# Gate of each layer: the residual's second half transposed on VectorE and moved by direct on-chip transfers, first projection unit between the gate's second and third unit

## The reference, cut to what matters

```python
h = h + mix                                            # the mixer's output
h = h + swiglu(rms_norm(h, norm_ffn[i]), ffn_w_in[i], ffn_w_out[i])
gate = jax.nn.sigmoid(rms_norm(h, ple_norm[i]) @ ple_w_gate[i])     # 1024 x 1024
h = h + gate * (p[i] @ ple_w_proj[i])                                # 256 x 1024
```

## Time and profile before

| what | value |
|---|---|
| median of three runs | 903.44 us (903.12 to 903.55) |
| the profiled execution's own time | 902.82 us |
| its span (first to last instruction) | 900.6 us |
| TensorE matmuls | busy 893.0 us (99%), 4358 instructions |
| VectorE | busy 654.4 us (73%), 995 instructions |
| ScalarE | busy 508.0 us (56%), 821 instructions |
| GpSimd | busy 62.3 us (7%) |
| SyncE's DMA queue | 182.99 MB, 60.2% of 16 engines |
| granted TensorE clock | 1.000 of full speed in the whole span |

### The profile page before, as it was taken

The page is one execution under the profiler, slowest core; times in us unless marked ns, Lnnn a source line. Parts: engine busy times, 40 slices in busy tenths (PEclk is TensorE's granted clock), DMA queues, the critical chain, the costliest instruction groups (busy, mean ns, idle before and its releaser), DMA issues.

```text
span 900.6 us, 12222 instructions
## 1 busy us (share of the span) xinstructions
PE 893.0 (99%) x4358; PEld 737.1 (82%) x4358; DVE 654.4 (73%) x995; ACT 508.0 (56%) x821; POOL 62.3 (7%) x75
## 2 busy tenths in 40 slices
PE   9999999999999999999999999999999999999998
PEld 8988888888888888778888888888888888887776
DVE  5985478777735699997787776646679897779663
ACT  6756555444444667688564444435664645587681
POOL 0001000000000003211100000000010000225100
PEclk9999999999999999999999999999999999999999
DMA  7674459777755666424487777746658775657611
GB/s 260 202 240 140 168 189 303 270 242 243 240 195 193 225 201 203 161 95 139 141 291 257 234 246 246 250 147 224 212 204 284 254 259 185 217 204 235 227 52 47
DMA packets 76844, 187.47 MB, mean 208 GB/s; under 512 B 6836, under 2 KB 31540, under 8 KB 76792
## 3 DMA queue, kind: packets, MB, share of 16 engines
q1 hardware_dynamic: 75336, 182.99, 60.2%
q0 software_dynamic: 1024, 3.15, 1.0%
q10 hardware_dynamic: 432, 0.66, 0.2%
HBM read 171.83 MB, written 14.94 MB: 207 GB/s over the span
## 4 chain that ended last, share of the span: by engine, by line
PE 94%; DMA 2%; DVE 2%; ACT 1%; issue 1%; ACTq 0%; DVEq 0%
PE bank L1792 84%; PE bank L1819 3%; DMA raw<-stream_dram 2%; PE bank L1834 1%; PE bank L2094 1%; PE bank L2120 1%; DVE wlo L1077 1%; PE bank L2204 1%; DMA h<-x_dram 0%; PE bank L2105 0%; PE bank L1941 0%; PE bank L1989 0%; PE bank L1993 0%; PE bank L2080 0%; PE bank L2214 0%
## 5 line engine op out<-in xcount | busy, mean ns | idle before, releaser
L669 ACT ACTIVATE whi<-raw 128x1024 fp32r<-128x1024 f32 x295 | 306.5, 1060 | 181.7 <-DMA raw<-stream_dram 104.6
L1077 DVE TENSOR_TENSOR wlo<-raw,whi 128x1024 fp32r<-128x1024 f32 x295 | 347.8, 1214 | 53.9 <-ACT whi L669 53.2
L1792 PE MATMUL bank<-whi,x_hi 128*128 128x512 f32 x560 | 152.5, 394 | 0.0
L1792 PE MATMUL bank<-wlo,x_hi 128*128 128x512 f32 x560 | 149.9, 389 | 0.0
L1792 PE MATMUL bank<-whi,x_lo 128*128 128x512 f32 x560 | 149.7, 389 | 0.0
L1792 PEld LDWEIGHTS bank<-wlo,x_hi 128*128 128x128 f32 x560 | 105.1, 188 | 22.1
L1792 PEld LDWEIGHTS bank<-whi,x_lo 128*128 128x128 f32 x560 | 105.1, 188 | 22.0
L1792 PEld LDWEIGHTS bank<-whi,x_hi 128*128 128x128 f32 x560 | 103.4, 188 | 21.8 <-issue 1.2
L1792 PE MATMUL bank<-whi,y_hi 128*128 128x512 f32 x400 | 109.5, 394 | 0.0
L1792 PE MATMUL bank<-wlo,y_hi 128*128 128x512 f32 x400 | 107.6, 389 | 0.0
L1792 PE MATMUL bank<-whi,y_lo 128*128 128x512 f32 x400 | 107.5, 389 | 0.0
(11 more groups left out here) (244 smaller groups left out, 886.0 us busy)
## 6 DMA issues: line engine op xcount, KB each, us to landing
raw<-stream_dram SPq DMA_DIRECT2D x295, 512.0 KB, 4.5
ffn_blocks<-ffn_blk SPq DMA_DIRECT2D x22, 256.0 KB, 2.0
ffn_land<-ffn_blocks SPq DMA_DIRECT2D x22, 256.0 KB, 4.0
second_blocks<-h_blk SPq DMA_DIRECT2D x8, 256.0 KB, 2.0
h_land<-second_blocks SPq DMA_DIRECT2D x8, 256.0 KB, 3.0
cv_blocks<-cv_blk SPq DMA_DIRECT2D x7, 256.0 KB, 5.2
cv_land<-cv_blocks SPq DMA_DIRECT2D x7, 256.0 KB, 3.5
h_blocks<-h_blk SPq DMA_DIRECT2D x3, 512.0 KB, 6.5
```

The lines of the kernel that those rows point to most:

```text
L669: A(whi[:, u % RING, :], raw[:, u % RAW, :], ACT.Copy).then_inc(sem("w_hi"), 1)
L1077: V.tensor_tensor(wlo[:, u % RING, :], raw[:, u % RAW, :], whi[:, u % RING, :].bitcast(F32), ALU.subtract).then_inc(sem("w_lo"), 1)
L1792: last = T.matmul(bank[pair + t][:, :], lhs[a][:, kt, t * P:(t + 1) * P], w[:, u % RING, kk * NW:(kk + 1) * NW], start=part != 1 and k == ...
```

## The change

The second half of the residual reaches the gate by blocks instead of through TensorE, and the blocks are moved inside the chip: `cross` issues four transfers for one piece, each from 32 partitions of `h_blk` (2 KB each) to 128 partitions of `h_land` (512 B each), 64 KB in all, with no DRAM tensor in between. The same transfers replace the way over DRAM in `second_blocks` (four uses before, six now) and in `gate_blocks` (two). The first half for the gate (`half_blocks`) still goes over DRAM. The units of `tple` and `tple+1` are made in the order of `GATE_ORDER`: gate 0, gate 1, projection, gate 2, gate 3.

```diff
+GATE_ORDER = ((0, 0), (0, 1), (1, 0), (0, 2), (0, 3))
...
+            for tile in (PLE0, PLE1):
+                for n, (t, k) in enumerate(GATE_ORDER):
+                    SOURCE[END[tile] + n] = END[tile + t] + k
...
+            def cross(dst, src, signal):
+                for i in range(P // B):
+                    sp.dma_start(dst[:, i, :], src[i * B:(i + 1) * B, :]).then_inc(sem(signal), 16)
...
                 for q in range(2):
                     sp.wait_ge(sem("g_blk"), 2 * r + q + 1)
-                    sp.dma_start(s_dram[s, q], sblk[:, q, :]).then_inc(sem(f"g_out{q}"), 16)
-                for q in range(2):
-                    sp.wait_ge(sem(f"g_out{q}"), 16 * (r + 1))
-                    sp.dma_start(sland[:, q, :, :], s_dram[s, q].rearrange("q n -> (q n)")
-                                 .rearrange("(i p w) -> p i w", i=P // B, p=P)).then_inc(sem(f"g_land{q}"), 16)
+                    cross(sland[:, q, :, :], sblk[:, q, :], f"g_land{q}")
...
                 for t in range(TT):
-                    sp.wait_ge(sem("g_blk"), 2 * (2 * n + 1) + t + 1)
-                    sp.dma_start(g_dram[n, t], gblk[:, t, :]).then_inc(sem(f"g_out{t}"), 16)
-                for t in range(TT):
-                    sp.wait_ge(sem(f"g_out{t}"), 16 * (2 * n + 2))
-                    sp.dma_start(gland[:, t, :, :], ...).then_inc(sem(f"g_land{t}"), 16)
+                    sp.wait_ge(sem("g_blk"), 2 * (3 * n + 2) + t + 1)
+                    cross(gland[:, t, :, :], gblk[:, t, :], f"g_land{t}")
...
                 done = half_blocks(n, tin + FT)
+                done = second_blocks(3 * n + 1, tin + FT + 2)
                 done = gate_blocks(n, tin + FT + 2)
... ScalarE
                 split_to(END[tple] + 1 + AHEAD)
-                lhs_hi(src, norm_gain(j), (6, 7))
                 squares(j, 1)
+                second_hi(j, src, 3 * n + 1, END[tple])
                 act.wait_ge(sem("rstd"), j + 1)
                 for half in range(2):
                     t = tple + 2 * half
-                    split_to(END[t + 1] + AHEAD - 2 * half)
-                    c.wait(act, "w_used", END[t + 1])
+                    over = END[t + 1 + (half == 0)]
+                    split_to(over + AHEAD - 2 * half)
+                    c.wait(act, "w_used", over)
... VectorE
                 residual(tout + 1, 1)
-                split_to(END[tout + 2] + 1 + AHEAD)
-                lhs_lo(src, norm_gain(j), (6, 7))
+                second_blk(12 * n + 6)
+                second_lo(j, src, 3 * n + 1, END[tple])
... TensorE
-                more2 = list(half0) + [None, None]
-                def second_half2():
-                    more2[2:4] = h_T(1, 3 * n + 2)
-                product(tple, src, "ple_sig", need=more2, hooks=[(1, second_half2)])
-                product(tple + 1, PT, "ple_gated", need=[("pT", 2 * (n + 1))])
+                more2 = list(half0) + second_need(3 * n + 1)
+                for at, (t, k) in enumerate(GATE_ORDER):
+                    product(tple + t, PT if t else src, "ple_gated" if t else "ple_sig" if k == 3 else None,
+                            need=[("pT", 2 * (n + 1))] if t else more2, only=k, at=END[tple] + at)
```

More of the change, by code:

```diff
@@ L527, in _ @@
                 done = END[out_tile]
-                done = second_blocks(2 * n, tin)
+                done = second_blocks(3 * n, tin)
                 fetch(done, done_at(tin) + 10)
@@ L532, in _ @@
                 done = half_blocks(n, tin + FT)
+                done = second_blocks(3 * n + 1, tin + FT + 2)
                 done = gate_blocks(n, tin + FT + 2)
-            done = second_blocks(4, CV_IN)
+            done = second_blocks(6, CV_IN)
             fetch(done, done_at(CV_IN) + 10)
@@ L549, in _ @@
             done = max(done, END[MB_IN])
-            done = second_blocks(5, MB_IN)
+            done = second_blocks(7, MB_IN)
             fetch(done, UNITS)
@@ L692, in mixer_lhs @@
                 squares(j, 1)
-                second_hi(j, dst, 2 * (j - 1) // 3, END[out + 4])
+                second_hi(j, dst, j - 1, END[out + 4])
             def second_hi(j, dst, r, base):
@@ L727, in next_lhs @@
                 squares(j, 1)
-                second_hi(j, dst, 5, END[first + 1])
+                second_hi(j, dst, 7, END[first + 1])
             def evacuate(tile, j, dst, width, signal, func=ACT.Copy, scale=None):
@@ L1144, in parts_out @@
                 second_blk(4 * (j - 1) + 2)
-                second_lo(j, dst, 2 * (j - 1) // 3, END[out + 4])
+                second_lo(j, dst, j - 1, END[out + 4])
             V.memset(warm[:, :], 0.0).then_inc(sem("warm"), 1)
@@ L2033, in ffn @@
                 other = Y if src is X else X
-                first_tiles(tin, src, "ffn_mid", list(got) + second_need(2 * n))
+                first_tiles(tin, src, "ffn_mid", list(got) + second_need(3 * n))
                 product(tin + 2, src, "ffn_mid")
@@ L2053, in ffn @@
                 half0 += [("h_lhs", 2 * n + 1), ("h_lhs", 2 * n + 2)]
[L2054 to L2060 removed]
+                more2 = list(half0) + second_need(3 * n + 1)
+                for at, (t, k) in enumerate(GATE_ORDER):
+                    product(tple + t, PT if t else src, "ple_gated" if t else "ple_sig" if k == 3 else None,
+                            need=[("pT", 2 * (n + 1))] if t else more2, only=k, at=END[tple] + at)
                 half1 = []
                 product(tple + 2, src, "ple_sig")
[L2063 removed]
+                half1 += [("g_lhs", 2 * (3 * n + 2) + k + 1, ("g_hi", 4 * (3 * n + 2) + k + 3)) for k in range(2)]
                 product(tple + 3, PT, "ple_gated")
@@ L2160, in cv_T @@
                 free[b] = ("cv_lhs", 8)
-            first_tiles(CV_IN, X, "cv_prod", list(half) + second_need(4))
+            first_tiles(CV_IN, X, "cv_prod", list(half) + second_need(6))
             product(CV_IN + 2, X, "cv_prod")
@@ L2268, in mb_beside @@
                         mb_zT(arg)
-            first_tiles(MB_IN, X, "mb_in", list(got) + second_need(5), mb_beside)
+            first_tiles(MB_IN, X, "mb_in", list(got) + second_need(7), mb_beside)
             for t in range(2, 8):
```

17 lines of the change are left out of this document (6 added, 11 removed).

## The result

The changed kernel takes 915.89 us (four runs, 915.46 to 915.97), the kernel before 903.28 us in the same comparison (902.45 to 903.55). The ratio is 1.014, with a 95% interval of 1.0128 to 1.0152: slower by 12.6 us. The forecast was 901.7 us, with a range from 900.7 to 903.1.

A forecast was written before the change was run, and what follows sets the result against it. TensorE's own stream was taken as the bound (busy 893.0 of 900.6 us). Profiled execution 902.82 - 1.77 (transposes) + 0.1 (given back) = 901.15, with the median of runs 0.62 above; forecast 901.7 us, range 900.7 to 903.1.

The forecast's parts named there:

- The projection unit only changes its place: Gate: moving the projection's twelve matmuls costs nothing; inputs are old, banks free three us before it starts.
- eight transposes per layer: TensorE at the gate: removing them saves 0.89 us in the first layer, 0.88 in the second, 1.77 together.
- The third gate unit is on time: Gate: first piece's lo part done at 309.34, 0.56 us before it is wanted; slow transfer costs at most 0.26.
- The hi part: First piece, third gate unit: ScalarE free at 306.6 decides, blocks landed at 305.8; done at 307.5, wanted at 308.09.
- an issue: SyncE in the gate's passage: eight direct issues of 0.35 us from 302.74, so free at about 305.7.
- The sigmoid was put at 314.0 to 314.6: First layer's gate: gate tile finished about 313.8, so the sigmoid starts 0.2 to 0.8 us late.
- u0+10: Weight unit fetched behind the transfers: released at 307.1, landed at 311.6 to 312.2, split by ScalarE before the sigmoid.
- I count 0.1 us given back in the first layer: Chain behind the sigmoid: VectorE ends at 327.0 to 327.6, next multiplication wanted at 327.63; 0.1 us lost.
- the weights come late: Rival: u0+10 lands 1 us or more later, TensorE waits for h at the next mixer; 902.6 us, chance 0.20.
- The slower rival: The four small transfers of a piece follow one another instead of overlapping; 943 us, chance 0.08.
- More falls than the transposes: Rival: TensorE's waits of 0.21 and 0.27 us beside the sigmoid chain fall too; 901.2 us, chance 0.12.
- The signs of being wrong: TensorE waiting for blocks in the third gate unit, for h over 1 us, or a span shorter by over 2.3.

The follow-up runs named there:

- order alone: Kernel before with only the projection unit moved between the gate's second and third unit; transposes and way over DRAM stay: 906.63 us, ratio 1.0039.
- old order: Changed kernel with four gate units, then the projection, and splits ahead of the sigmoid ending at u0+9: 908.26 us, ratio 1.0056.
- Over DRAM: Changed kernel with all direct transfers replaced by the way over DRAM: 914.56 us, ratio 1.0116.
- other banks: Changed kernel with the first gate tile accumulated in the unused banks 4 and 5: 911.84 us, ratio 1.0086.
- earlier sigmoid: Changed kernel with ScalarE splitting two weight units fewer before the sigmoid: 904.47 us, ratio 1.0015.
- a fetch between: Changed kernel with SyncE fetching one weight unit (u0+8) between the two pieces' issues in the gate's passage: 912.64 us, ratio 1.0104.

## Why the prediction was wrong, step by step

- **The failed step:** "The projection unit only changes its place: same twelve matmuls, no cost. Its inputs are old (the turned p) and its banks are free". I checked the banks of the unit that moves, not those of the tile that then follows `tple` at once. The order alone costs 1.40 us per layer, 906.63 against 903.03 us, and with the late sigmoid and the low clock the price becomes 7.6 in the first layer (wait 4.92, clock 2.7), of which the transposes give back 0.89.
- **Right:** eight transposes per layer fall, with unbroken spacing (299.89 to 312.58). The third gate unit is on time: lo part done at 309.06 (forecast 309.34), 8.97 us after the residual's start (8.98). The hi part starts at 306.53 (306.6), but that fit is luck: ScalarE was to be free last, at 306.6, and the blocks to land at 305.8; in fact ScalarE was free at 305.36 and waited 1.17 us for the landing. In the second layer 0.2 us of wait remain, for the same landing. The fit was bought by the projection unit in the middle, as the old order shows.
- **Sizes off:** an issue takes 0.60 us, not 0.35, and eight of them 5.08 us (forecast 2.8), so SyncE was free at 307.54, not 305.7. The sigmoid was put at 314.0 to 314.6 and started at 317.21. The term that was off is u0+10: I had it issued on its release at 307.1 and landed 4.5 to 5.1 us later. It is the third of the fetches bunched behind 307.59, so it is issued at 308.71, 1.6 us late, and its split starts at 314.84, when it has landed, some 6.1 us later. Over DRAM it is issued sooner and lands as late. "I count 0.1 us given back in the first layer" rested on that sum, and it asked only whether VectorE's next product would come late, never who waits for the banks.
- **The rivals:** "the weights come late" had the right cause and the wrong victim. I priced it through h at the next mixer (up to 0.9 us); it hit the claim inside the gate first. With other banks it does hit the next mixer, with 3.46 us, also by a claim rather than by h. The slower rival, transfers one after another, did not come: 64 landings of 2.1 us in the median, issued some 0.64 us apart, so they overlap. "More falls than the transposes" did not come either: the wait for h at the next mixer is 0.35 us, before 0.27.
- **The signs of being wrong** named a wait for the blocks, a wait for h and a shorter span. The wait that came is none of the three, as the claim of the banks was not on the list of what TensorE can wait for.
- **The clock** had no term, since it was 1.000 before. It is 5 of the 13 us.
- With the claim and the lateness both taken away, the kernel takes 901.84 us, faster than before at 0.998 (0.9972 to 0.9989): within 0.2 us of the forecast. That is close partly by chance, as this kernel has other banks and fewer splits ahead of the sigmoid than the one that was forecast.

The Trainium skill's rule of about 2 us fixed per transfer ("DMA: Bandwidth & Descriptors", anatomy of one DMA, fitted there to transfers that GpSimd issues) agrees with these landings from SyncE, 2.1 us for 64 KB, as a latency. Of the 8 of 16 ports that the Trainium skill gives partitions 0 to 31 ("SBUF — State Buffer", DMA port swizzle), no run here shows whether they cost anything: a transfer of the same size and kind that reads from all partitions was not run beside it.

## What to carry to other kernels

Before moving a product in TensorE's order, write down for the product that then follows which accumulator banks it takes, who reads them last, and what TensorE did in the meantime; a short independent product between two tiles of the same banks is cover, and it can't be moved for nothing. When a chain (here the sigmoid) is late, look for every claim behind it, since removing the first wait may only move it to the next. And price a new wait of TensorE with the clock that it loses afterwards.

## What the runs showed of the hardware that was not expected

- **Clock after a wait.** Waits of 1.40 us (order alone; earlier sigmoid), 1.69 us (earlier sigmoid, second layer) and 2.00 us (old order, first layer) left the granted clock at its full level. After waits of 2.22 us (old order, second layer), 3.06 and 3.47 (a fetch between), 3.46 and 3.81 (other banks), 4.50 and 4.92 (changed kernel), 3.93 and 5.05 us (over DRAM) it stood at 0.50 for the following 3 to 6 us. The waits of 2.00 and 2.22 us are one of each, in one execution.
- **Issue time on SyncE.** 0.60 us per direct transfer from 32 partitions, 0.42 us for 32 partitions to DRAM, against 0.28 and 0.32 for the small transfers of the earlier trace rows, 0.33 for most fetches and 0.43 to 0.59 for the four fetches in a row.
- **GpSimd's small operations stretch.** In the second layer of the changed kernel an operation on 128x2 elements (L576) took 3.52 us and in the first layer 1.31, both while VectorE was splitting; in the kernel before the same operation took 0.20 us in the first layer, with VectorE idle, and with the old order it took 0.20 beside VectorE's splits too. It lies off the path, and its cause was not looked into.
